# Two 4-byte parts instead of three 2-byte parts in the gate products of an expert layer

## The reference, cut to what matters

```python
e = i_first * N_KEYS + i_second                    # 128 experts of each token, out of 16384
gw = softmax(best)                                 # their weights
act = gelu(einsum('tkd,td->tk', u_tab[e], xb)) * gw
return einsum('tk,tkd->td', act, v_tab[e])
```

## Time and profile before

| | us |
|---|---|
| median of 3 runs | 2125.3 (2123.61 to 2126.17) |
| profiled execution | 2125.43 |
| its span, first to last instruction | 2123.7 |
| busy: TensorE, VectorE, ScalarE, GpSimd | 1988.3, 1379.6, 710.1, 683.0 |

### The profile page before, as it was taken

The page is one execution under the profiler, slowest core; times in us unless marked ns, Lnnn a source line. Parts: engine busy times, 40 slices in busy tenths (PEclk is TensorE's granted clock), DMA queues, the critical chain, the costliest instruction groups (busy, mean ns, idle before and its releaser), DMA issues.

```text
span 2123.7 us, 29266 instructions
## 1 busy us (share of the span) xinstructions
PE 1988.3 (94%) x10901; PEld 1619.7 (76%) x10901; DVE 1379.6 (65%) x2488; ACT 710.1 (33%) x946; POOL 683.0 (32%) x466
## 2 busy tenths in 40 slices
PE   6999877696899999999999999979999999999998
PEld 4998454445888788888888878868888888888886
DVE  4252549344198879678957977636666666666676
ACT  3113117321133444355345434433222222222222
POOL 2001200010145665466456546623222222212221
PEclk9999988898999999999999999989999999999999
DMA  8243834621234697489559748889988888888882
GB/s 317 83 55 65 282 127 158 213 84 51 68 126 154 213 347 292 134 302 349 184 196 351 290 144 289 323 320 364 318 291 285 295 283 298 279 299 288 282 294 102
DMA packets 215811, 488.26 MB, mean 230 GB/s; under 512 B 31320, under 2 KB 99416, under 8 KB 210464
## 3 DMA queue, kind: packets, MB, share of 16 engines
q1 hardware_dynamic: 176112, 319.13, 45.7%
q0 software_dynamic: 36864, 134.23, 17.5%
q10 hardware_dynamic: 2736, 33.60, 3.9%
HBM read 410.07 MB, written 76.57 MB: 229 GB/s over the span
## 4 chain that ended last, share of the span: by engine, by line
PE 65%; DVE 5%; POOL 1%; DMA 1%; ACT 1%; issue 1%; SPq 0%; ACTq 0%; POOLq 0%; DVEq 0%
PE experts_ps L1741 33%; PE experts_ps L1722 28%; PE experts_ps L1733 4%; POOL u_low L182 1%; DMA token_gates<-scratch_G 1%; PE experts_ps L1710 1%; DVE whot L1999 1%; DVE s_vr L1995 0%; ACT u_high L1805 0%; DVE keyb L1981 0%; DVE gather_rows L1972 0%; DVE oN L1956 0%; DVE oN L1953 0%; DVE experts_ps L2063 0%; DVE picks L1959 0%
## 5 line engine op out<-in xcount | busy, mean ns | idle before, releaser
L182 POOL TENSOR_TENSOR u_low<-u_raw,u_high 128x1024 fp32r<-128x1024 f32 x128 | 325.1, 2540 | 297.2 <-ACT u_high L1805 192.0
L1722 PE MATMUL experts_ps<-h2h,u_high 128*128 128x512 f32 x1024 | 408.2, 399 | 7.4 <-POOL u_low L182 7.4
L1741 PE MATMUL experts_ps<-s_vh,s_ah 128*128 128x512 f32 x1024 | 399.7, 390 | 10.8 <-DVE s_al L2015 10.8
L1722 PE MATMUL experts_ps<-h2h,u_low 128*128 128x512 f32 x1024 | 400.3, 391 | 0.0
L1741 PE MATMUL experts_ps<-s_vh,s_al 128*128 128x512 f32 x1024 | 399.5, 390 | 0.0
L1722 PE MATMUL experts_ps<-h2l,u_high 128*128 128x512 f32 x1024 | 399.4, 390 | 0.0
L1741 PE MATMUL experts_ps<-s_vl,s_ah 128*128 128x512 f32 x1024 | 399.3, 390 | 0.0
L1602 POOL DMA_INDIRECT gather_rows<-in_v_tab,expert_index x128 | 154.7, 1209 | 529.7 <-DVE u_raw L2024 504.2
L2013 DVE TENSOR_TENSOR s_vl<-s_vr,s_vh 128x1024 fp32r<-128x1024 f32 x128 | 156.7, 1224 | 209.1 <-ACT s_vh L1829 209.1
L1829 ACT CAST s_vh<-s_vr 128x1024 fp32r<-128x1024 f32 x128 | 134.8, 1053 | 466.7 <-PE experts_ps L1741 448.8
L1741 PEld LDWEIGHTS experts_ps<-s_vh,s_ah 128*128 128x128 f32 x1024 | 192.9, 188 | 51.3 <-issue 11.2
(11 more groups left out here) (342 smaller groups left out, 2692.4 us busy)
## 6 DMA issues: line engine op xcount, KB each, us to landing
u_raw<-in_uT SPq DMA_DIRECT2D x128, 512.0 KB, 4.0
s_vr<-in_v_tab SPq DMA_DIRECT2D x128, 512.0 KB, 4.6
scratch_HG<-s_ar SPq DMA_DIRECT2D x128, 256.0 KB, 4.2
scratch_G<-token_gates ACTq DMA_DIRECT2D x16, 2048.0 KB, 11.0
s_ar<-scratch_HG SPq DMA_DIRECT2D x128, 256.0 KB, 3.7
token_gates<-scratch_G SPq DMA_DIRECT2D x32, 1024.0 KB, 10.1
wa<-in_w_ada SPq DMA_DIRECT2D x10, 2048.0 KB, 8.2
past_k<-in_cache_kT SPq DMA_DIRECT2D x8, 1024.0 KB, 8.0
```

The costliest lines, as they stand in the source:

```text
L182: eng.tensor_tensor(self.low[:, s, :, :], self.raw[:, s, :, :], self.high[:, s, :, :].bitcast(F32), ALU.subtract).then_inc(self.low_done, 1)
L1722: mm = pe.matmul(hP[:, slot, :], w[:, slot, k, :], x[:, k, 0:SEQ], start=(k == 0 and w is u.high and x is m.h2h), stop=(k == KD - 1 and w ...
L1741: mm = pe.matmul(yP[:, y, :], a[:, s, t * P:(t + 1) * P], v[:, s, d], start=(start and a is ah and v is vh), stop=(stop and v is vl))
```

## The change

The gate weights are cut into two parts of float32r instead of three of bfloat16 (`NW = 2`), and the one-hots are float32r too: `hot` now takes all of `vr` and `whot` grows from 12 to 16 KB a partition. The keys aren't cast any more, the comparison reads them from `picksT`; `rest` lies over `cab`. A round now makes its weight parts with a cast, a subtraction and a cast. A step has two weighted one-hots instead of three, and a token two products instead of three. The waits between the engines stay.

```diff
@@ -1491,7 +1491,7 @@
 SLOTS = H * TOPK
 NGAT = 4
 UN = 8
-NW = 3
+NW = 2
 EV = UN // 4
 STEPS = P // UN
 HS = HT // UN
@@ -1502,6 +1502,7 @@
 
 
     def __init__(self, nc, sb):
+        self.v_at = next_at(nc)
         self.v, self.a = sb("s_vr", [P, GB, D]), sb("s_ar", [P, GB, SEQ])
         self.rows = sb("gather_rows", [P, NGAT, D])
         self.gate_at = next_at(nc)
@@ -1529,17 +1530,18 @@
     zs, rz = sb("zs", [P, H]), sb("rz", [P, H])
     picksT = sb("picksT", [P, 3, P])
     iota16 = sb("iota16", [P, TOPK])
-    iota = sb("iota", [P, NKEY, 2], BF16)
-    keyb, wb, rest = sb("keyb", [P, 2, P], BF16), sb("wb", [P, NW, P], BF16), sb("rest", [P, NW - 1, P])
-    whot = sb("whot", [P, 2, NW, UN // 2, NKEY, 2], BF16)
+    iota = sb("iota", [P, NKEY])
+    wb, rest = sb("wb", [P, NW, P], F32R), cab[:, 0, :, :].bitcast(F32).rearrange("p h r -> p (h r)")
+    whot_at = next_at(nc)
+    whot = sb("whot", [P, 2, NW, UN // 2, NKEY, 2], F32R)
     index, slot_w = sb("expert_index", [P, SLOTS], U32), sb("slot_weight", [P, SLOTS])
     slot_h, slot_a = sb("slot_h", [P, SLOTS]), sb("slot_act", [P, SLOTS])
     vr, ar, rows, Gs = wide.v, wide.a, wide.rows, wide.gate
-    hot = vr[:, 0:2, :].bitcast(BF16).rearrange("p b (c u k w) -> p b c u k w", c=2, u=UN // 2, w=2)
     ga = ar[:, 2:4, :]
     flat_gate = Gs[:, :, :].rearrange("p j t -> p (j t)")
     gr = flat_gate[:, 0:NKEY * HT].rearrange("p (g t n) -> p g t n", g=2, t=NHT)
     over = lambda name, at, shape, dt=F32R: nc.alloc_sbuf_tensor_at(name, shape, dt, offset=at)
+    hot = over("hot", wide.v_at, [P, 2, 2, UN // 2, NKEY, 2])
     ah = over("s_ah", wide.gate_at + 4 * NKEY * HT, [P, GB, SEQ])
     al = over("s_al", wide.gate_at + 4 * (NKEY * HT + GB * SEQ), [P, GB, SEQ])
     vh, vl = over("s_vh", m.qhT_at, [P, GB, D]), over("s_vl", m.oN_at, [P, GB, D])
@@ -1548,7 +1550,7 @@
     u = m.u
     own = u.raw[:, :, :, :].rearrange("p s k c -> p s (k c)")
     result = lambda t: yP[:, 2 * t:2 * t + 2, :].rearrange("p a n -> p (a n)") if t < ND else own[:, 0, :]
-    res_post = whot[:, :, :, :, :, :].bitcast(F32).rearrange("p b k u j w -> p (b k u j w)")[:, 0:D]
+    res_post = over("res2_post", whot_at, [P, D], F32)
     setup, zeroed, keys_in = sem("route_setup"), sem("route_zeroed"), sem("keys_in")
     s_made, s_taken = sem("rs_made"), sem("rs_taken")
     stepA, stepB, stepC = sem("routeA"), sem("routeB"), sem("routeC")
@@ -1588,7 +1590,7 @@
         with nc.Block() as block:
             @block.gpsimd
             def _(pool):
-                pool.iota(iota[:, :, :], pattern=[[1, NKEY], [0, 2]], base=0, channel_multiplier=0,
+                pool.iota(iota[:, :], pattern=[[1, NKEY]], base=0, channel_multiplier=0,
                           allow_small_or_imprecise_dtypes=True).then_inc(setup, 1)
                 pool.iota(iota16[:, :], pattern=[[1, TOPK]], base=0, channel_multiplier=0,
                           allow_small_or_imprecise_dtypes=True).then_inc(setup, 1)
@@ -1976,27 +1978,24 @@
                     return spread(v[:, q * UN:(q + 1) * UN].rearrange("p (g w) -> p g w", w=2), 2, NKEY)
 
                 def one_hots(r):
-                    p0 = (r - 1) * (2 * NW)
+                    p0 = (r - 1) * 3
                     dve.wait_ge(t_taken, r)
-                    dve.tensor_copy(keyb[:, :, :], picksT[:, 0:2, :]).then_inc(parts, 1)
                     dve.tensor_copy(wb[:, 0, :], picksT[:, 2, :]).then_inc(parts, 1)
-                    for k in range(1, NW):
-                        whole = picksT[:, 2, :] if k == 1 else rest[:, k - 2, :]
-                        dve.wait_ge(parts, p0 + 2 * k)
-                        dve.tensor_tensor(rest[:, k - 1, :], whole, wb[:, k - 1, :], ALU.subtract).then_inc(parts, 1)
-                        dve.wait_ge(parts, p0 + (2 * k + 1))
-                        dve.tensor_copy(wb[:, k, :], rest[:, k - 1, :]).then_inc(parts, 1)
-                    dve.wait_ge(parts, p0 + 2 * NW)
+                    dve.wait_ge(parts, p0 + 1)
+                    dve.tensor_tensor(rest, picksT[:, 2, :], wb[:, 0, :].bitcast(F32), ALU.subtract).then_inc(parts, 1)
+                    dve.wait_ge(parts, p0 + 2)
+                    dve.tensor_copy(wb[:, 1, :], rest).then_inc(parts, 1)
+                    dve.wait_ge(parts, p0 + 3)
                     for q in range(STEPS):
                         n, b = (r - 1) * STEPS + q, q % 2
                         if n >= 2:
                             dve.wait_ge(g_made, (n - 1) * EV)
                         for c in (1, 0):
-                            dve.tensor_tensor(hot[:, b, c, :, :, :], spread(iota[:, :, :], 1, UN // 2), pairs(keyb[:, c, :], q),
+                            dve.tensor_tensor(hot[:, b, c, :, :, :], spread(spread(iota[:, :], 1, UN // 2), 3, 2), pairs(picksT[:, c, :], q),
                                               ALU.is_equal).then_inc(hot_done, 1)
                         dve.wait_ge(hot_done, n * 2 + 1)
                         for k in range(NW):
-                            op = dve.tensor_tensor(whot[:, b, k, :, :, :], hot[:, b, 1, :, :, :], pairs(wb[:, k, :], q), ALU.mult)
+                            op = dve.tensor_tensor(whot[:, b, k, :, :, :], hot[:, b, 1, :, :, :].bitcast(F32), pairs(wb[:, k, :].bitcast(F32), q), ALU.mult)
                         op.then_inc(whot_done, 1)
                         dots(n)
```

## The result

| | kernel before | changed kernel |
|---|---|---|
| median | 2125.45 (4 runs) | 2173.1 (4 runs, 2166.68 to 2178.14) |
| profiled execution | 2125.43 | 2178.14 |
| its span | 2123.7 | 2176.4 |

The changed kernel takes 1.0218 times as long, with a 95% interval of 1.02 to 1.0235. In a second set of runs, on another occasion, it had a median of 2166.91 against 2125.66: 1.0208, interval 1.019 to 1.0227. So it is 41 to 48 us slower, where the prediction had +32.

A forecast was written before the change was run, and what follows sets the result against it. TensorE bounds mid-round steps, with a VectorE-GpSimd chain just under it. Round starts 10.9, 48 later steps 19.7 and last gate sets 1.6 sum to +32.2 on 2125.3, giving 2158; range 2138 to 2190.

The forecast's parts named there:

- VectorE's passes: One-hot passes in each step: from 0.605 to 1.14 each, four instead of five, +1.54 per step.
- TensorE's product: Gate products: 16 of 4 bytes at 111 ns replace 24 at 57.5, set 1.78, +0.40 per step; bounds 57.5 and 222.
- The step: One hidden block plus one gate set, mid-round: 6.92 becomes 7.33, +0.41, TensorE and VectorE-GpSimd chains coming out alike.
- the second chain: VectorE's one-hots, GpSimd's subtraction, hidden block, gate set: 14.66 in two steps, 7.33 each; 1.1 slack before.
- The floor of 7.13: VectorE's two-input passes and GpSimd's subtraction don't run together, so next one-hots start no sooner than 7.13 after the last.
- GpSimd's gathers: Two gathers (0.96 for one) must fit between GpSimd's subtractions; 4.9 is left, enough even at twice that length.
- The starts of rounds: Second hidden block's subtraction comes 2.35 later in round 2; starts of all four rounds add 10.9.
- The last gate sets: Last gate set of each round, 4 x 0.40 = 1.6 more.
- the price of plain fp32: Rival on gate products: each takes 222 ns, step 9.09, +140, 2265; chance 0.10.
- load and stream one after the other: Rival on gate products: 168 ns each, step 8.23, +87, 2212; chance 0.06.
- load hidden: Rival: weight load hidden wholly or partly, gate products at 57.5 to 80 ns, 2132 to 2143; chance 0.06.
- The other side: Rival: cost goes by elements, not bytes; products stay 57.5, passes 0.605, step 6.46, -30, 2095; chance 0.03.

The follow-up runs named there:

- contiguous_spread: Changed kernel with gate-product operands read with step 1 and the gates sent to memory in quarters; 2156.74, ratio 1.0137.
- contiguous: Changed kernel with one-hots of neighbouring tokens no longer interleaved, so TensorE reads both gate-product operands with step 1 instead of 2; 2162.03, ratio 1.0178.
- one_product: Changed kernel with one gate product a token on TensorE instead of two, VectorE's work the same; 2161.26, ratio 1.0159.
- spread_store: Changed kernel with gates stored in 512 KB quarters, one behind each step, instead of 2048 KB behind every fourth; 2166.24, ratio 1.0205.
- after_again: The changed kernel run once more without edits, for a second profile (the repeated kernel); 2166.91, ratio 1.0208.
- two_parts_fp16: Kernel before with two float16 weight parts instead of three of bfloat16; keys and one-hots float16 too; 2094.59, ratio 0.9848.

## Why the prediction was right, and what it missed

The time lay inside the range, slower as forecast; the size was too small, +32 for +41 to +48. This is the sum by its parts, against the stage as read from the starts of the gate sets (us more than before):

| | forecast | changed kernel, two profiles | `contiguous_spread` |
|---|---|---|---|
| first three steps of each round | 10.9 | 13.8, 14.0 | 10.2 |
| the other 48 steps | 19.7 | 31.6, 29.8 | 21.0 |
| last gate sets, and between rounds | 1.6 | 0.2, 0.2 | 0.1 |
| sum | 32.2 | 45.5, 44.1 | 31.3 |

By its own steps:

- **VectorE's passes**, 1.14 apart from 0.605: two take 963.08 - 960.78 = 2.30 to the next, as said, and 1234 and 1216 ns answer to the row that was taken (1224).
- **TensorE's product** was mis-sized. The prediction took 111 from plain fp32 records and said that no row shows whether a step of 8 bytes slows TensorE. It does, to 119: the set takes 1.91 for the 1.78 of the sum, the step 7.44 for 7.33, 5.6 over the 48 steps. With contiguous operands the 111 is what was measured. The bounds, 57.5 and 222, held it.
- **The step**: 7.33 forecast, 7.44 measured, 7.34 in `contiguous`, where the second chain holds it. That two chains come out alike was right: take away VectorE's pass and TensorE holds 7.40, take away half of the products and the step is 6.97, half of the second chain. One slip in the working changes little: 1.53 - 23 x 0.0575 is 0.21, not 0.23, and a 4-byte product's own length is 0.30 here (0.27 in `contiguous`).
- **The floor of 7.13** was right in kind and some 0.15 too high (`one_product`). It holds for the passes that make one-hots (1.33 to 1.375 for 1.22 where they begin 0.24 to 0.29 ahead) and for the passes of 2048 elements shown there (4.37 for 2.29), not for every pass of two inputs: the dot products run beside the subtraction (959.00 to 961.36 against 959.17 to 961.57) at their usual 1.22; one of their operands lies in `experts_ps`. In the forecast's own case the floor didn't bind.
- **GpSimd's gathers**: "4.9, enough" asked only whether GpSimd has the time to issue them, not when they land behind the store. The margin was hardly there before: a gather issued at 961.72 is used by the first dot product two steps on, at 959.00 + 2 x 6.92 = 972.84, 11.1 later, and the longest landing that the trace has was 10.9. After the change GpSimd issues them later against the end of the gate products, so that the second one sets out 0.5 to 1.0 ahead of the store instead of 2.1. This was a wait that the prediction didn't have: 4.6 to 6. That the store is the reason is shown by `spread_store`; that the nearness of the two issues is, is argued from the eleven slow gathers of the first profile.
- **The starts of rounds**: the stand of 2.13 in round 2 answers to "some 2 longer", and without slow blocks the starts come to 10.2 for 10.9 (`contiguous_spread`). The slower first block, held for possible in the range but at nothing in the sum, is the third missed term: 1.6 in round 2 of the first profile, 1.6 in each of rounds 2 and 3 of the repeated kernel (7.35 for 5.74). Over the five profiles with four passes of VectorE and two products a token (the repeated kernel counted too) it came in seven of ten such starts, after stands of 2.13 to 2.26.
- **The last gate sets**: the 1.6 didn't come. From a round's last set to the next round's first it is as far as before (80.89, 80.85, 73.67 before; 80.67, 81.00, 73.47 in `after_again`). This made up for some of what was missed.
- **The rivals**: the price of plain fp32, load and stream one after the other, and load hidden are all out, by the 119 of the changed kernel and the 111 of `contiguous`. The other side (cost by elements, not by bytes) is out too, but its number, 2095, is what `two_parts_fp16` gives, since that keeps the elements at 2 bytes. The 80 ns at the upper end of load hidden was the author's assumption; no run shows it, the runs have 57.5 for 2-byte and 108 to 120 for 4-byte operands.

Three terms were missed, then: the dearer product, the late rows and the slow blocks. With the first two taken away and the third by chance not there, the sum comes out at 31.3 for 32.2, and the time at 2156.74 for 2158 (`contiguous_spread`). That it comes so near is in part luck.

## What to carry to other kernels

## What the runs showed of the hardware

- A 4-byte product of the split format with 128 columns repeats every 111 ns with contiguous operands (`contiguous`), every 119 with a step of 8 bytes in both (changed kernel); the 2-byte one repeats every 57.5 with a step of 4 bytes (kernel before, `two_parts_fp16`).
- A one-input cast of 128 elements waited out GpSimd's subtraction (2.20 for 0.23). A two-tensor pass of 1024 elements that began 0.16 before such a subtraction ended was hardly longer (2.37 for two, usually 2.36), and one that began 0.24 before was (2.46). The dot product, with one operand in `experts_ps`, ran beside it at its usual 1.22.
- A gather of table rows issued 0.5 to 1.0 before a store of 2048 KB landed 12.0 to 14.2 after its issue (eleven in the changed kernel); with the store in quarters the longest took 9.9 (`spread_store`).
- A stand of TensorE of 2.13 was followed by a granted clock of 0.70 over the next 4 us in round 2 of the changed kernel, and by one of 1.00 in round 3.
- The stretch ahead of the expert layer, the same in both kernels, ended between 580.9 and 592.2 in profiles of one kernel.
